# Where the products of the decayed keys stand within a pair of heads of a delta-rule recurrence

## What is computed

```python
def step(S, inp):
    r_t, w_t, k_t, v_t, a_t, b_t = inp
    sa = jnp.einsum('bhvk,bhk->bhv', S, a_t)
    S = (S * w_t[:, :, None, :] + sa[..., None] * b_t[:, :, None, :]
         + v_t[..., None] * k_t[:, :, None, :])
    return S, jnp.einsum('bhvk,bhk->bhv', S, r_t)
```

## Time and profile before

| | us |
|---|---|
| median of 3 runs | 1087.32 |
| lowest and highest of them | 1084.68, 1091.79 |
| the profiled execution | 1088.06 |
| its span, first to last instruction | 1086.3 |
| TensorE busy (PE) | 1047.9, 96% of the span |
| VectorE busy | 649.0, 60% |
| ScalarE busy | 455.2, 42% |

### The profile page before, as it was taken

One profiled execution on the slowest core, in us unless ns is written; L12 is line 12 of the kernel. 1 busy time (PEld: TensorE's weight loads), 2 busy tenths in 40 slices (PEclk: granted clock), 3 DMA queues, 4 the chain that ended last, 5 costly groups with the idle time before them and its releaser, 6 DMA issues.

```text
span 1086.3 us, 22599 instructions
## 1 busy us (share of the span) xinstructions
PE 1047.9 (96%) x9830; PEld 826.4 (76%) x9830; DVE 649.0 (60%) x1019; ACT 455.2 (42%) x738; POOL 5.6 (1%) x10
## 2 busy tenths in 40 slices
PE   8999998988999999999999999999999999999998
PEld 6777776776787777777777767787888888888887
DVE  4569898966467665868676747564443323444322
ACT  5344554677325543443444236344442112443111
POOL 0000000000000000000000000000000000000000
PEclk9999999999999999999999999999999999999999
DMA  9812124000522210110101121142233232333230
GB/s 361 360 63 97 59 97 173 3 2 3 193 103 75 76 40 22 41 39 24 41 24 40 42 79 42 50 145 97 97 97 99 96 97 96 97 97 97 97 107 30
DMA packets 26161, 95.01 MB, mean 87 GB/s; under 512 B 2896, under 2 KB 3152, under 8 KB 25552
## 3 DMA queue, kind: packets, MB, share of 16 engines
q1 hardware_dynamic: 26064, 93.57, 24.9%
HBM read 89.36 MB, written 4.19 MB: 86 GB/s over the span
## 4 chain that ended last, share of the span: by engine, by line
PE 75%; DVE 15%; ACT 4%; issue 3%; DMA 2%; SPq 1%; POOL 0%; ACTq 0%; DVEq 0%
PE psum L842 19%; PE psum L844 18%; PE psum L843 18%; DVE work L2008 4%; PE psum L852 3%; DMA ring<-weights 2%; PE psum L1271 2%; PE psum L1258 2%; PE psum L1027 1%; DVE small_temps L2195 1%; PE psum L1330 1%; PE psum L983 1%; PE psum L1307 1%; DVE in_weights_low L2064 1%; PE psum L1284 1%
## 5 line engine op out<-in xcount | busy, mean ns | idle before, releaser
L2064 DVE TENSOR_TENSOR weights_low<-ring,weights_high 128x1024 fp32r<-128x1024 f32 x70 | 85.8, 1226 | 75.4 <-ACT weights_high L1618 75.4
L1618 ACT ACTIVATE weights_high<-ring 128x1024 fp32r<-128x1024 f32 x70 | 73.6, 1052 | 127.5 <-PE psum L844 127.5
L842 PE MATMUL psum<-normed_high,weights_high 128*128 128x512 f32 x256 | 100.1, 391 | 0.2 <-DVE weights_low L2064 0.2
L844 PE MATMUL psum<-normed_high,weights_low 128*128 128x512 f32 x256 | 99.6, 389 | 0.0
L843 PE MATMUL psum<-normed_low,weights_high 128*128 128x512 f32 x256 | 99.6, 389 | 0.0
L842 PE MATMUL psum<-hidden_high,weights_high 128*128 128x512 f32 x256 | 99.6, 389 | 0.0
L843 PE MATMUL psum<-hidden_low,weights_high 128*128 128x512 f32 x256 | 99.6, 389 | 0.0
L844 PE MATMUL psum<-hidden_high,weights_low 128*128 128x512 f32 x256 | 99.6, 389 | 0.0
L2008 DVE SCALAR_TENSOR_TENSOR work<-work,small_sb 128x512 f32<-128x512 f32 x116 | 80.0, 744 | 0.1
L1588 ACT ACTIVATE work<-psum 128x384 f32<-128x384 f32 (+1 forms) x116 | 56.8, 539 | 50.8 <-PE psum L983 20.8
L842 PE MATMUL psum<-pair_normed_high,pair_weights_high 128*128 128x512 f32 x176 | 75.5, 429 | 0.8 <-DVE normed_low L2068 0.8
(11 more groups left out here) (319 smaller groups left out, 2126.7 us busy)
## 6 DMA issues: line engine op xcount, KB each, us to landing
ring<-weights SPq DMA_DIRECT2D x135, 512.0 KB, 3.7
work<-weights SPq DMA_DIRECT2D x10, 512.0 KB, 13.0
residual<-xT SPq DMA_DIRECT2D x4, 512.0 KB, 6.6
mixed<-weights SPq DMA_DIRECT2D x4, 512.0 KB, 6.8
residual_saved<-residual SPq DMA_DIRECT2D x8, 256.0 KB, 4.5
residual<-residual_saved SPq DMA_DIRECT2D x1, 2048.0 KB, 9.0
outT<-residual SPq DMA_DIRECT2D x8, 256.0 KB, 3.3
tables_sb<-tables SPq DMA_DIRECT2D x1, 1280.0 KB, 13.0
```

The lines of the kernel that those rows point to most:

```text
L842: pe.matmul(out, wh, high(k), start=first and n == 0, stop=False)
L844: ins = pe.matmul(out, wl, high(k), start=False, stop=last and n == len(order) - 1)
L1618: act.activation(wsplit(q)[0], room_of(b), ACT.Copy).then_inc(w_high, 1)
L2064: vec.tensor_tensor(low, room_of(b), high.bitcast(F32), ALU.subtract).then_inc(w_low, 1)
```

## The change

The products `ka` are taken out from between `na` and the turns and put behind the first level's products with the inverse (`y2` for both heads), ahead of what stood between these and the first update. The wait for the decayed keys goes to the turn of the keys (`tk`), which is now the first to read them. The list of the banks follows; `ka` keeps banks 6 and 7. The queues of the other engines are unchanged.

```diff
@@ psum_order
-        o.extend([(f"nf_{p}", 2, 0), (f"na_{p}", 2, 2), (f"ka_{p}", 2, 6)])
+        o.extend([(f"nf_{p}", 2, 0), (f"na_{p}", 2, 2)])
         o.extend((f"{x}_{p}", 1, n) for n, x in zip((0, 1, 4, 5), ("ta", "tb", "tk", "tv")))
         for n, b in enumerate(LEVELS):
             first = n % 2 * 2
             o.extend((f"y{b}_{p}_{h}", 1, first + h) for h in range(HEADS))
+            if n == 0:
+                o.append((f"ka_{p}", 2, 6))
@@ tensor
                 key_products(f"na_{p}", p, B[p % 2])
-                pe.wait_ge(kd_ready, p + 1)
-                key_products(f"ka_{p}", p, KD[p % 2])
                 v3 = V0.rearrange("p (c t) -> p c t", c=NC)
                 for x, src in (("ta", AR[p % 2][:, 0]), ("tb", B[p % 2]), ("tk", KD[p % 2]), ("tv", v3)):
+                    if x == "tk":
+                        pe.wait_ge(kd_ready, p + 1)
                     if x == "tv":
                         pe.wait_ge(*is_free(f"v_{p}"))
                     turn_pairs(f"{x}_{p}", src)
@@ tensor, in the loop over the levels
                         times_inverse(f"y{b}_{p}_{h}", h)
 
+                    if b == LEVELS[0]:
+                        key_products(f"ka_{p}", p, KD[p % 2])
                     if p == NP - 1:
                         if b == LEVELS[0]:
                             gn_mean(p - 1)
```

## The result

| | before | after |
|---|---|---|
| median, us | 1086.56 | 1089.47 |
| lowest to highest | 1084.68 to 1091.79 | 1086.84 to 1091.4 |
| runs | 22 | 22 |
| the profiled execution (its span) | 1088.06 (1086.3) | 1090.52 (1088.7) |

The ratio is 1.0021, with a 95% interval of 1.0013 to 1.003: the changed kernel takes 2.3 us more (1.4 to 3.3). The medians alone lie 2.9 apart; wherever this text gives a difference with a range, it is worked out from the ratio. The forecast was 2.3 us more.

A forecast was written before the change was run, and what follows sets the result against it. The prediction took VectorE's queue, not TensorE, to set `x2` in the middle pairs. Six pair terms (0.65 + 0.45 + 0.46 - 0.65 + 0.45 + 0.95) gave +2.3 us, forecasting 1089.6; 8-in-10 range 1084.8 to 1094.8.

The forecast's parts named there:

- pair 0: Opening of pair 0: the old place was idle anyway, the new one has 0.24 us to fill; +0.65 us.
- pairs 1, 2, 4: Middle openings: turns 0.16 us earlier, but `ka` outlasts the 0.33 us idle before `x2`; +0.45, +0.46, +0.45 us.
- pair 5: Opening of pair 5: nothing comes back at the turns and no idle follows `y2`, so `ka` is bare; +0.95 us.
- What bounds the opening: Middle pairs: VectorE's queue of masks and sums, not TensorE, sets the start of `x2`; pair 2's cannot precede 494.46.
- The turns: First turns wait for VectorE's second mask in all six pairs, starting 0.05 us after it; 6.2 to 6.5 us waiting.
- What `ka` costs in its new place: Between `y2` and `x2`: `ka` takes 0.95 us, 0.33 fills idle time and 0.62 pushes `x2` later.
- Pair 3's stop: Before pair 3's turns, a late instruction block costs 1.21 us; the new order hides it: -0.65 us, else +0.45.
- Rival 1: Same mechanism, but the stop without a semaphore is kept or moves to another pair: +3.4 us, 1090.7; chance 0.33.
- Rival 2: Instruction supply gains all over and both stops go: +1.0 us, 1088.3; chance 0.12 together with Rival 5.
- Rival 3: `ka` fills nothing behind `y2`, and small products make a stop in each of pairs 0 to 4: +7.6 to +10; chance 0.10.
- Rival 5: No effect, since `ka` ends before the level mask anyway: 1087.3 us; chance 0.12 together with Rival 2.
- Rival 4: Longer TensorE standstills halve the clock, doubling the pairs' openings: about +40 us, 1128; chance 0.02.

The follow-up runs named there:

- after_again: The second comparison: the changed kernel, unaltered, run again beside 35 runs of the kernel before on the same chip; 1088.61 against 1087.36 us, ratio 1.0011.
- banks_swapped: Changed kernel with `ta`, `tb` in banks 4 and 5 and `tk`, `tv` in 0 and 1; 1087.78 us against 1086.52 for the kernel before, ratio 1.0015.
- products_twice: Kernel before with `ka` computed twice, in its old place and again in the new one; 1089.98 against 1086.52 us, ratio 1.0034.
- stream_shift: Kernel before with 144 already satisfied waits (72 TensorE instructions) added ahead of all pairs; 1088.26 against 1086.52 us, ratio 1.0017.
- pair_3: Kernel before with `ka` moved in pair 3 alone; 1085.72 against 1086.9 us, ratio 0.9992.
- pairs_1_to_4: Kernel before with `ka` moved in pairs 1 to 4 only; 1086.18 against 1087.36 us, ratio 0.999.
- pair_0: Kernel before with `ka` moved in pair 0 alone; 1087.5 against 1087.36 us, ratio 1.0.
- r_late: Kernel before with VectorE's decayed `r` of pair 1 made in pair 0's second level, not ahead of its masks; 1086.37 against 1086.9 us, ratio 0.9992.
- combined: Kernel before with `ka` moved in pair 3, the mean's sum moved in pairs 1, 2, 4, and decayed `r` late; 1085.56 against 1086.9 us, ratio 0.999.

## Why the prediction was right, point by point

**The total.** Forecast +2.3, measured +2.3 (1.4 to 3.3) and, in the second comparison, +1.2 (0.2 to 2.1). The direction, the kind of each term and the gain in pair 3 were right. That the number was hit to the tenth is luck: the forecast's own six terms measure 1.5 in the openings, and the executions with a clock of 1.00 on one chip give 1.5 as well. What lies above that in the first comparison are things that the sum held at nothing: short stops such as the one of pair 0, and perhaps falls of the clock. The 1% (10.9 us) that the prediction took for the finest difference that can be told was also far too wide; 22 runs a side gave 0.2% with a range of 0.1% to either side.

| term | forecast | measured in profiles |
|---|---|---|
| pair 0 | +0.65 | +0.54 in the opening, +0.89 in the pair |
| pairs 1, 2, 4 | +0.45, +0.46, +0.45 | +0.30 to +0.31 (0.35 and 0.41 in one profile) |
| pair 3 | -0.65 | -0.80 in the opening, -0.87 in the pair |
| pair 5 | +0.95 | +0.88 |
| clock | 0 | 1.6 for a fall, in some executions |

**What bounds the opening.** That VectorE's queue and not TensorE's sets the middle pairs held in its hardest test: `banks_swapped` took the wait for the banks away and the time stayed. The page Perfetto Trace Analysis of the Trainium skill (section Optimizing Tensor Performance, Matmuls), which asks that the next group cover the emptying of banks, would have given 5.7 us; the runs give +2.3 and +1.2.

**The turns.** Forecast from 0.05 us after the mask, measured 0.06; waits of 6.2 to 6.5 us in six pairs, measured 5.8. The middle pairs show 0.64 where 0.7 to 0.8 was said, because the printed idle counts from the modelled end of `na`'s last record (1.10 long, not 0.95). The distance from `na` to the turns, 1.75 against 1.74 forecast, is the sounder figure.

**What `ka` costs in its new place.** Right in kind, mis-sized: the step that lets the next group start 1.0 after `y2` and then adds 0.95 for `ka`. From `y2` to `x2` 1.95 were forecast and 1.68 measured; from `na` to `x2` of pair 2 5.59 forecast and 5.33 measured, 0.20 above before. Groups of small products overlap at their borders: `ka`'s first record starts at 495.75, before the last of `y2`, and the first `x2` in pair 0 of `after_again` at 397.35, before the last of `ka`. The same 0.26 is what pair 3 gained beyond its forecast up to `x2`. Part of this is only how early a first record starts; at the second level, where all has passed, 0.31 is left of the 0.46. `products_twice` gives both halves: 0.46 for the new place (0.62 forecast), 0.16 back at the old one (0.16 forecast).

**Pair 3's stop.** It was read from 79 packets of 16 KB and a row of idle time without a semaphore, and a moved block was inferred. `stream_shift` bears it out: 72 instructions more move the stop by 72 instructions, and the count over all profiles puts every such stop at the same distance from a multiple of 256. That it was hidden in the new order was right in both profiles of the changed kernel and in `pair_3` and `pairs_1_to_4`. The reason given, that the block has 0.9 us more because TensorE waits for VectorE first, fits but was not tested apart from the place itself. One reading was wrong without effect: GpSimd makes the decayed keys for pair 1 too, not for pair 0 alone, and TensorE waited for them in no pair.

**Rival 1** (the stop moves to another pair) came in small in the changed kernel itself: at 401.54 us in pair 0 (0.18 printed), and in `after_again` at the same block's end (0.35 lost). At full size (0.57 to 0.93 in pair 0) it came in `pair_0`, `banks_swapped`, `r_late` and `combined`, elsewhere in `stream_shift` and `products_twice`. It was the likelier thing than its 0.33 against 0.42 made it look: the position of such a stop can be counted, its size in an execution could not be foretold. **Rival 2** counted the stop at 473 us as one the change could remove. It is missing in the profile after and present in `after_again`, with the same program, so its swing of 1.16 us belongs to the execution. **Rival 3** was wrong: `ka` does fill idle time, and with the move in all pairs no middle pair had a stop in its opening. **Rival 5** was refuted by the 0.3 in each pair.

**Rival 4** (the clock) was given 0.02 because the clock stayed at 1.00 with an idle of 1.22. That step failed for pair 0, whose idle of 2.2 was in the forecast: the clock fell in the profiled execution. What was wrong in the price is the form: a fall lasts 3.4 us and costs 1.6, not 40. Whether the changed kernel has more falls is open. In the first comparison only 4 of its 22 executions had a mean clock of 1.00, but the clocks of the 22 before are not on record. In the second it was 5 of 11 against 15 of 35 on the same chip, no fewer. With the order at 1.5 us, up to 0.8 of the first comparison's 2.3 could be falls; that is an estimate.

**What stays open.** Why the end of a block shows as a stop in one execution and is hidden in the next of the same program, as at 473 us, was not tried. A transfer that is under way at that moment, or the state of the instruction queue, are both possible. Nor is it known how often the clock falls after a standstill of 2.10 us.

## What to carry to other kernels

When a group is moved into idle time, price both ends: what it covered where it stood, and how much of it is longer than the hole; here 0.95 us of products went into 0.33 us of idle time, and gave back 0.16, while 0.6 us of other sums, whose old place covered nothing, gained 0.3 in the same hole. Before you free a bank or take away a wait, look at what the next engine's queue ends with: here the idle time moved there, 0.64 us becoming 0.60. An edit in a stream of dense small products also moves which product lies at the end of an instruction block; a shift alone gave +1.8 us, so count the positions of the stops before you credit a gain or a loss of 1 us to the edit. And compare executions at the same mean clock: one fall is as large as the whole effect here.

## What the runs showed of the hardware

- TensorE's longer stops without a semaphore lie on a grid of 256 instructions: all 18 of 0.48 to 1.33 us, in twelve of fourteen profiles, stand 193 or 194 instructions behind a multiple of 256 by the count of the traces. Most ends of blocks show no stop.
- Satisfied waits alone, 72 instructions ahead of the recurrence, gave +1.8 us (0.7 to 2.9 by the ratio's interval), though the recurrence started no later: stops of 0.6 to 1.1 us came at other places of the work.
- The granted clock falls from 1.00 to 0.50 (2.4 to 1.2 GHz) in single pieces of 3.413 us. Of 94 executions of the kernel before 39 had a mean of 1.00 (mean time 1085.7 us), 44 had 0.998 (1087.4) and 8 had 0.997 (1089.3): the first step is 1.6 us and the next 2.0. A mean of 0.998 is one such piece in 1086 us, and this count is a large part of the spread of this kernel's runs; three chips stand in the pool.
- A fall followed a standstill of TensorE of 2.10 us in one of three profiles, and one of 3.96 us in the single profile there is. Five of fourteen profiles have a fall near 686 us, where the kernel before's longest idle shortly before it was 0.73 us.
- The stop at 473 us is absent in one execution of the changed kernel and 1.33 us long in another; five of fourteen profiles have it.
